# Attention stage: ScalarE copies a transposed gate ahead of the exponentials of its step

## What the reference computes

```python
p = jnp.exp(s - m)                                    # group A, s has the sink's maximum in m
w = p / (jnp.sum(p, axis=-1, keepdims=True) + jnp.exp(sk - m))
oa = jnp.einsum('...hgqk,...khd->...qhgd', w.astype(v.dtype), v)
...
w = jax.nn.softmax(s, axis=-1)                        # group B, s is -inf where a key was not picked
ob = jnp.einsum('bqhgk,bqkhd->bqhgd', w.astype(v_all.dtype), vg)
...
y = jnp.concatenate([oa * jax.nn.silu(ga), ob * jax.nn.silu(gb)], axis=-1)
```

## Time and profile before

| | |
|---|---|
| median of 3 runs | 5151.94 us (5150.16 to 5154.29) |
| the profiled execution | 5151.13 us |
| its span, first to last instruction | 5149.3 us |
| TensorE, ScalarE, VectorE, GpSimdE busy | 85%, 67%, 68%, 31% of the span |
| attention stage, us from the span's start | about 2,505 to 4,547 |

### The profile page before, as it was taken

One profiled execution on the slowest core, in us unless ns is written; L12 is line 12 of the kernel. 1 busy time (PEld: TensorE's weight loads), 2 busy tenths in 40 slices (PEclk: granted clock), 3 DMA queues, 4 the chain that ended last, 5 costly groups with the idle time before them and its releaser, 6 DMA issues. The chain is left out here.

```text
span 5149.3 us, 78325 instructions
## 1 busy us (share of the span) xinstructions
PE 4358.7 (85%) x26505; PEld 2723.9 (53%) x26505; DVE 3487.5 (68%) x6644; ACT 3454.5 (67%) x6887; POOL 1618.2 (31%) x1358
## 2 busy tenths in 40 slices
PE   6767777777677786877689999989999999989999
PEld 3434443434333343434366777767777777754444
DVE  1266778888797898989477777786676768625111
ACT  1578888988787797873388888868788885520100
POOL 1345566667657856777310000000000000000000
PEclk9888889888788888888799999999999999999999
DMA  6211111100011111101421111011010010034423
GB/s 142 68 44 44 37 38 36 38 30 34 27 40 40 37 36 41 41 32 44 155 72 61 43 45 44 28 53 39 26 42 25 28 40 24 12 113 138 115 97 102
DMA packets 201975, 276.98 MB, mean 54 GB/s; under 512 B 50496, under 2 KB 134176, under 8 KB 201056
## 3 DMA queue, kind: packets, MB, share of 16 engines
q1 hardware_dynamic: 198624, 271.81, 16.9%
q10 hardware_dynamic: 2960, 0.17, 0.0%
HBM read 156.73 MB, written 114.16 MB: 53 GB/s over the span
## 5 line engine op out<-in xcount | busy, mean ns | idle before, releaser
L595 PE MATMUL bank<-w,x 128*128 128x512 f32 (+1 forms) x2848 | 1248.7, 594 | 23.9 <-DVE w L940 12.9
L1042 DVE TENSOR_SCALAR_CACHE_REDUCE ties<-score,cand 128x512 int8<-128x512 f32 (+13 forms) x448 | 1110.6, 2479 | 123.1 <-POOL score L916 107.8
L595 PEld LDWEIGHTS bank<-w,x 128*128 128x128 f32 x2848 | 573.1, 205 | 607.2 <-issue 541.4
L806 ACT ACTIVATE act_junk<-score,a_cand,a_sign 128x384 int8<-128x384 f32 (+13 forms) x420 | 879.4, 2094 | 14.0
L613 PE MATMUL bank<-kiT,qi 128*128 128x512 f32 (+3 forms) x1136 | 400.4, 495 | 409.6 <-DVE kiT L960 204.2
L1832 DVE CUSTOM_DVE_ANT_0 row<-bank,mask 128x512 f32<-128x512 f32 (+3 forms) x1024 | 622.6, 639 | 180.5 <-PE bank L1571 179.4
L1538 POOL TENSOR_TENSOR near_bias<-table,mask 128x2048 f32<-128x2048 f32 (+1 forms) x32 | 129.5, 4047 | 1789.8 <-DVE part L1832 1773.7
L1766 ACT ACTIVATE pT<-bank 128x512 f32<-128x512 f32 (+2 forms) x704 | 368.3, 523 | 455.6 <-PE bank L1587 453.7
L1668 ACT ACTIVATE row<-row,top 128x1024 f32<-128x1024 f32 (+7 forms) x640 | 632.9, 990 | 4.0 <-DVE top L1845 4.0
L1587 PE MATMUL bank<-ident,row 128*128 128x128 f32 x4224 | 597.3, 282 | 25.3 <-DVE pT L1943 19.5
L1571 PE MATMUL bank<-kT,qb 64*128 64x256 f32 (+1 forms) x4352 | 609.0, 397 | 8.1 <-DVE part L1832 4.7
(11 more groups left out here) (255 smaller groups left out, 4894.9 us busy)
## 6 DMA issues: line engine op xcount, KB each, us to landing
qk_t<-ring SPq DMA_DIRECT2D x66, 256.0 KB, 2.0
gates<-ring SPq DMA_DIRECT2D x66, 256.0 KB, 2.0
gate<-gates SPq DMA_DIRECT2D x33, 512.0 KB, 3.4
out<-x_in SPq DMA_DIRECT2D x33, 512.0 KB, 2.9
x<-in_x_prompt SPq DMA_DIRECT2D x32, 512.0 KB, 3.7
mixed<-mixT SPq DMA_DIRECT2D x64, 256.0 KB, 2.0
mix_in<-mixed SPq DMA_DIRECT2D x32, 512.0 KB, 4.3
x_in<-in_x_prompt SPq DMA_DIRECT2D x32, 512.0 KB, 3.9
```

The lines of the kernel that those rows point to most:

```text
L595: ins = pe.matmul(p_bank[n % 2][:, 0:n1 - n0], held[:, c * P:(c + 1) * P], w[:, c, n0:n1], start=(c == 0), stop=(c == KC - 1))
L806: tick(act.activation(junk, row, ACT.Sign, bias=c, scale=back, accum_out=a_sum[:, :]))
L1042: n = tick(dve.tensor_scalar(ties[:, 0:width], row, c.bitcast(F32), 0.0, ALU.is_ge, ALU.add, accum_out=counts[:, i:i + 1]))
```

## The change

In ScalarE's loop the gate copy of a step moves from behind the exponentials of that step to ahead of them. It stays behind the copy of the turned half 0, and the parts of the late search stay last. No instruction is added or removed, and no other engine's program changes. The last gate copy, after the loop, is untouched.

```diff
                     act.activation(pT[0][at % 2][:, 0:cols], t_bank[0][:, 0:cols], ACT.Copy).then_inc(s_c0, 1)
-                    for x in PLAN[n, g]:
-                        exponential(*x)
                     for kind, m, j in PLACED[n, g]:
                         if kind == "gate":
                             copy_gate(m, j)
+                    for x in PLAN[n, g]:
+                        exponential(*x)
                     for _ in range(LATE_ACT[n, g]):
                         next(late_work, None)
```

## The result

| | median | lowest to highest | runs |
|---|---|---|---|
| before | 5150.84 us | 5141.69 to 5161.32 | 22 |
| after | 5160.47 us | 5150.21 to 5169.29 | 22 |

The ratio is 1.0017, with a 95% interval of 1.0011 to 1.0024: 8.8 us more (5.7 to 12.4). The change makes the kernel slightly slower, inside the band of 0.2% in the prediction's middle and inside its range.

What follows compares the result with a forecast made beforehand. TensorE was taken as the bound, paced by ScalarE's string of work around group A's turnings. Release gains nothing; added waits of 3.3 + 1.5 + 0.4 = 5.2 us, say +5, give a median of 5157 us, range 5147 to 5170.

Steps and rivals of the forecast that it cites:

- the band of 0.2%: Whole kernel: about 10 us is what a measurement can tell from no change; a result inside it had chance 0.77.
- Which string sets the pace: Group A's turnings, shown in tile 31: ScalarE's gapless string sets TensorE's pace, with TensorE waits of 0.94 and 0.16 us.
- VectorE's release: Steps (6t,0): gate multiplication up to 1.35 us earlier, TensorE's 0.35 us wait goes, but the next turning waits for ScalarE; gain nothing.
- The added wait: Steps (6t,0): ScalarE idles until TensorE has transposed the gate, making TensorE late; 3.3 + 1.5 + 0.4 = 5.2 us.
- 2 to 11 by its bounds: Range of the +5 us forecast, chance 0.55; rows cited: 0 us below (no wait, tile 21), 11.5 us above.
- faster rival: Before group A's turnings: VectorE's release saves TensorE's 0.35 us wait in some 20 tiles, 7 us, giving 5145; chance 0.10.
- ScalarE's wait of L1676: Sign, attention stage: ScalarE's gate copy waiting for TensorE's gate transposes (L1626) rises from 12.1 us by about 8.
- TensorE's wait for VectorE before group A's turnings: Sign, attention stage: this wait, 15.0 us before the change, falls by about 7 us.
- Tile 31's turning: Sign, the turning at 4460.26 in tile 31: TensorE waits about 1.6 us ahead of it.
- TensorE's wait for ScalarE there: Sign, before group A's turnings: this wait, 40.8 us before the change, rises by about 7 to 12 us.
- The clock: Rival, tiles 4 to 31: merged TensorE waits drop its clock in 10 to 24 more tiles, 13 to 31 us extra; chance 0.20.
- The sign that I had named for the clock: Steps (6t,0) to (6t+2,0), tiles 4 to 31: more than eight of the 28 stretches below granted clock 1.00.

Runs made afterwards that it cites:

- e4: Kernel before, old gate order, but from tile 8 on job 6t+3's exponentials go to the steps of job 6t+2 alone: 0.9930, 36 us faster.
- e9: Changed kernel, with TensorE repeating the two transposes of half 1 in step (6t+1,0) three more times: 0.9997 of the kernel before, -2 us.
- e3: Changed kernel, with TensorE turning the gate of step (6t,0) later, behind the values of the step before: 1.0071 of the kernel before, +37 us.
- e8: Changed kernel with the gate turned later, plus three more repeats of half 1's two transposes in step (6t+1,0): 1.0029 of the kernel before, +15 us.
- e10: Kernel before, old gate order, plus three more repeats of half 1's two transposes in step (6t+1,0): 1.0003 of the kernel before, +2 us.
- e7: Kernel before, with the gate copy moved ahead of the exponentials in all tiles but 4, 8, 20 and 24 to 31: 1.0008, +4 us.
- e2: Kernel before, old gate order, with TensorE turning the gate of step (6t,0) later, behind the values of the step before: 1.0000, 0 us.
- e6: Kernel before, with the gate copy moved ahead of the exponentials only in tiles 4, 8, 20 and 24 to 31: 1.0017, +9 us.
- e1: Kernel before, but in steps (6t,0) the gate copy stands behind the first exponential and its sink, ahead of the second: 1.0010, +5 us.

## Why the prediction was right, and what it missed

**Which string sets the pace: right.** VectorE's release was forecast to be worth nothing, because the turning behind it waits for ScalarE. VectorE's wait fell by 33.1 us (more than 30 forecast) and no stretch became shorter by it. e4 shows the reason from the other side.

**The added wait: right, in place and size.** The sum was 5.2 us; in the stretches at full clock it measures 4.95. Two numbers around that sum were wrong: the lower edge in "2 to 11 by its bounds" has no row, since the row that it names gives 0, and half of the faster rival's 7 us under 5152 leads to 5148.5, not 5147.

| tiles | forecast, each | measured, each, at full clock |
|---|---|---|
| 24 to 31 | 0.41 | 0.38 to 0.50 |
| 4, 8, 20 | 0.5 | 0.44 to 0.45 |
| 14, 16, 19 (of five that share 0.4) | 0.08 | 0.10 to 0.15 |
| all others from 4 on (tile 7 forecast at 0.08) | 0 | 0, within 0.02 |

Tiles 0 to 3, ahead of the stretch sum, took 92.9 us against 93.6 together. ScalarE's wait of L1676 rose by 8.7 us (about 8 forecast) and TensorE's wait for VectorE before group A's turnings fell by 9.4 (about 7). Tile 31's turning waits 1.50 us (about 1.6).

**TensorE's wait for ScalarE there: undersized.** I forecast 7 to 12 us more, and it was 18.9. 9.4 of them came over from VectorE and about 5 are the wait. The rest I had left out: without VectorE's wait between them the four transposes run as one group, 0.66 us instead of twice 0.44, and so TensorE arrives still earlier. In the time this is nothing, since that group's busy time fell by 5.3 us.

**The clock: a rival that should have been a term.** I gave +5, with the clock as it was, 0.55, and 10 to 24 more falls 0.20, and had nothing between. What came lies between: +8.8 us, of which the wait is 4.95, and some 4 (1 to 7 by the interval) are left. That the total still lies inside the forecast's 2 to 11 is luck, since the 11 was worked out from waits of ScalarE alone. The sign that I had named for the clock, more than eight stretches below 1.00, didn't show either: there were six. That the rest is the clock is supported by e9, where filling TensorE's wait, with ScalarE's waits unchanged, brings the time back to that of before, and by e3 and e8, where the same filling takes 22 us and 18 falls.

A fall is dear enough, and has to be counted to the first step of the next tile, since it goes on behind its stretch. Tile 24 of the changed kernel so takes 3845.14 - 3753.77 = 91.37 us, and in e9 3849.33 - 3759.54 = 89.79: 1.58 us for one fall, of which 0.65 are inside the stretch. Five of the six cost 1.29 to 1.62 us in this way and tile 31's, counted to the end of the stage, 1.6, together 8.75; the four of the kernel before cost 1.29 to 2.04 each against e10, together 6.10. So I should have added a term of a few us to the sum: the prediction saw that idle time would be gathered into one wait, and that such a wait can cost a fall of 1.3 us.

The Trainium skill, "TensorE: Matmul & The Clock Gate", section "HAM oscillation — how this bites in real kernels", describes a loop whose waits for data, several us long, throw TensorE back to its lower clock in every pass. Here the longest wait of tile 31's stretch is 1.50 us and the clock fell there all the same, but only in some of the passes: 6 of 28 in the changed kernel, 18 in e3, where the waits are longer, and ten in e7, where they are shorter than in the changed kernel. Neither "none" nor "all" would have forecast that.

**What stays open.** The two profiled executions differ by 6.95 us from the first step of tile 4 to the end of the stage (1945.21 and 1952.16 us), and the falls make 8.75 - 6.10 = 2.65 of it. The other 4.3 are the wait, 4.95 in the stretches, with tile 20 some 0.6 us shorter behind its stretch. Some 2 us of the 8.8 are in no profile here; the changed kernel's profiled execution is among its fastest. The same holds for the 10 us that e9 gains on the changed kernel: in the profiles it is 8.9 us shorter from tile 4 on and 6.3 longer ahead of it. That more falls in the other executions make up the difference is likely and not shown. The clock granted over the whole span, a mean of all timed executions, agrees with it: 0.918 in the changed kernel and 0.921 filled, 0.914 in e3 and 0.921 in e8, 0.918 to 0.919 in the kernel before and 0.919 filled. Counting falls in one execution each, tiles with the old order in the kernels before, e2, e6 and e7 have 17 of 84 and tiles with the new or e1's order in after, e1, e6 and e7 have 25 of 84, which suggests the direction and no more. Why the filled kernel before still falls in three tiles, and which of a tile's waits makes it fall, I can't say.

## What to carry to other kernels

Ask of the engine that is to be released whether anyone waits for it next, and of the engine that does the releasing what it covers with the work that is moved: here 1.35 us of exponentials hid a wait, and since ScalarE works through its string in order, the wait that came out went straight through to TensorE. If one engine's string sets the pace of a stretch, shortening that string is worth far more than reordering it: 36 us for moving exponentials to where ScalarE has time, in e4, while the orders of e1 and e7 and the change itself gained nothing. And where an edit gathers TensorE's idle time, put a few falls of the clock into the sum as a term, and test them by filling that time with repeated work.

## What the runs showed of the hardware

TensorE's granted clock fell within stretches of 9 to 12 us whose single waits are short (in tile 31 after 0.32 and 1.50 us for ScalarE), and one fall cost 1.3 to 1.6 us in the changed kernel, counted to the first step of the next tile. Six more f32 transposes of 128x128 in such a wait (four run together take 0.66 us) took the falls from 18 to 0 and from 6 to 0 of 28 in the two kernels with the new order, 22 and 10 us of time, though TensorE did more work and tiles 0 to 3 became 4 to 6 us longer. They didn't in the kernel before, which kept 3. The spread between executions goes with the granted clock, taken over the whole span: over the changed kernel's 22 the two have a correlation of -0.78; the one at 5150.21 us had a mean of 0.921, those at 5164.81 and 5169.29 had 0.915 and 0.916.
